# The second input projection of a two-layer encoder as one unrolled stream, with its normalisation read back and its head scales on ScalarE

## What is computed

```python
def odd_layer(x, g_pre, g_post, w_in, q_norm, k_norm, w_out):
    ...
    h = rms_norm(x, g_pre)
    proj = jnp.einsum('btd,de->bte', h, w_in)
    q, k, v, gate = jnp.split(proj, SPLIT_C, axis=-1)
    q = rms_norm(q.reshape(B, T, C_HEADS, C_HEAD_DIM), q_norm)
    k = rms_norm(k.reshape(B, T, C_KV_HEADS, C_HEAD_DIM), k_norm)
    v = v.reshape(B, T, C_KV_HEADS, C_HEAD_DIM)
    q = jnp.concatenate([rope(q[..., :half], rows), rope(q[..., half:], cols)], axis=-1)
    k = jnp.concatenate([rope(k[..., :half], rows), rope(k[..., half:], cols)], axis=-1)
    q = q.reshape(B, T, C_KV_HEADS, C_HEADS // C_KV_HEADS, C_HEAD_DIM)
    o = block_attention(q, k, v, C_HEAD_DIM ** -0.5).reshape(B, T, C_WIDTH)
    y = jnp.einsum('bte,ed->btd', o * jax.nn.silu(gate), w_out)
    return x + rms_norm(y, g_post)
```

## Time and profile before

| | us |
|---|---|
| median of 3 runs | 2465.69 (2465.58 to 2466.36) |
| the profiled execution | 2463.42 |
| its span in the trace | 2461.6 |
| PE busy in the span | 2148.5 (87%) |
| DVE, ACT, POOL busy | 1582.5, 991.0, 1124.1 |
| granted PE clock, mean | 0.928 |

### The profile page before, as it was taken

How to read it: one execution, slowest core, us unless ns; L and a number is a source line. 1 busy time by engine, 2 the same in 40 slices (tenths; PEclk the granted TensorE clock), 3 DMA queues, 4 the chain that set the end, 5 groups by cost and what they waited for, 6 DMA issues and landing times. The chain is left out here.

```text
span 2461.6 us, 25658 instructions
## 1 busy us (share of the span) xinstructions
PE 2148.5 (87%) x9420; PEld 1600.6 (65%) x9420; DVE 1582.5 (64%) x1980; ACT 991.0 (40%) x1259; POOL 1124.1 (46%) x580
## 2 busy tenths in 40 slices
PE   6999988959999999958952987998699999996895
PEld 4777867847777766636742765787466666663674
DVE  7264156756776666625658999995377777773565
ACT  5132133213555566533323232210066666664331
POOL 5333443423555565523126767543266666663300
PEclk9999999977999999978976998999799999998898
DMA  4133487246555554244332222221623232313434
GB/s 154 35 118 129 128 295 192 73 118 126 116 117 112 115 114 99 59 133 140 99 106 83 78 94 98 82 94 65 149 50 82 65 75 65 73 39 112 157 103 128
DMA packets 223272, 262.75 MB, mean 107 GB/s; under 512 B 137440, under 2 KB 147040, under 8 KB 223152
## 3 DMA queue, kind: packets, MB, share of 16 engines
q1 hardware_dynamic: 223152, 261.17, 38.2%
HBM read 162.62 MB, written 98.50 MB: 106 GB/s over the span
## 5 line engine op out<-in xcount | busy, mean ns | idle before, releaser
L1689 POOL TENSOR_TENSOR c_PL<-c_PF,c_PH 128x1024 fp32r<-128x1024 f32 x128 | 307.0, 2399 | 199.1 <-ACT c_PH L1553 142.2
L1689 POOL TENSOR_TENSOR ab_PL<-ab_PF,ab_PH 128x1024 fp32r<-128x1024 f32 (+3 forms) x128 | 269.1, 2102 | 237.1 <-ACT ab_PH L1553 178.8
L1550 ACT ACTIVATE ab_PF<-ab_SA 128x1024 f32<-128x1024 f32 (+3 forms) x160 | 143.6, 897 | 243.6 <-PE ab_SA L1409 143.1
L1550 ACT ACTIVATE c_PF<-c_SA 128x1024 f32<-128x1024 f32 x160 | 164.3, 1027 | 168.7 <-PE c_SA L1444 168.7
L1601 DVE TENSOR_REDUCE c_MH<-c_SM 128x1 f32<-128x512 f32 x256 | 172.9, 688 | 85.2 <-PE c_SM L1374 83.6
L847 PE MATMUL e_acc<-e_XH,e_wh 128*128 128x512 f32 x480 | 197.8, 412 | 25.6 <-DVE e_XL_r L1016 16.1
L340 PE MATMUL p_acc<-XH,p_wh 128*128 128x512 f32 x432 | 186.4, 431 | 26.3 <-POOL Y_r L174 26.3
L847 PE MATMUL e_acc<-e_XL_r,e_wh 128*128 128x512 f32 x480 | 193.5, 403 | 0.0
L847 PE MATMUL e_acc<-e_XH,e_wl 128*128 128x512 f32 x480 | 193.4, 403 | 0.0
L340 PE MATMUL p_acc<-Y_r,p_wh 128*128 128x512 f32 x432 | 172.2, 399 | 0.0
L340 PE MATMUL p_acc<-XH,p_wl 128*128 128x512 f32 x432 | 172.1, 398 | 0.0
(11 more groups left out here) (255 smaller groups left out, 5569.9 us busy)
## 6 DMA issues: line engine op xcount, KB each, us to landing
o_G<-silu_gate SPq DMA_DIRECT2D x48, 256.0 KB, 2.8
c_Q<-qC_hi SPq DMA_DIRECT2D x32, 384.0 KB, 5.4
e_raw<-in_w_tiles SPq DMA_DIRECT2D x20, 512.0 KB, 3.8
p_raw<-in_w_tiles SPq DMA_DIRECT2D x18, 512.0 KB, 3.6
o_WL<-in_w_out SPq DMA_DIRECT2D x16, 512.0 KB, 5.6
e_XL<-in_xT SPq DMA_DIRECT2D x12, 512.0 KB, 9.8
silu_gate<-e_ta SPq DMA_DIRECT2D x24, 256.0 KB, 2.0
ab_Q<-qA_hi SPq DMA_DIRECT2D x16, 384.0 KB, 5.6
```

Source lines behind the costliest of these rows:

```text
L1550: nc.scalar.activation(used(PF[p], h, s), used(SA, h, s), ACT.Exp).then_inc(e_done, 1)
L1689: nc.gpsimd.tensor_tensor(used(PL[p], h, s), used(PF[p], h, s), used(PH[p], h, s).bitcast(F32), ALU.subtract).then_inc(p_lo[0], 1)
```

## The change

`project` is gone and a new function `inner` takes its place. It is written like `entry`: plain Python lists of units, no hardware loops.

- `output_projection` 0 no longer works out the next layer's norm, and ends as `output_projection` 1 does. `inner` does not take `Y` from SBUF. It loads x from `x_mid`, splits the raw values and sums the squares as `entry` does; the norm enters when DVE moves a unit out of PSUM (L1131 of after).
- The first six units take the first two weight tiles with the three chunks as they arrive. The head sums of unit 0 come after unit 6. From there two are done after each odd unit and one after each even one, until they run one unit behind.
- The head scale is ACT's: Ln of the mean square (L1032), then Exp with factor -0.5 (L1035). There is no reciprocal on DVE for it.
- POOL multiplies a weight tile by the gain once, in place (L856); ACT rounds it (L1001), POOL subtracts (L864).
- The values are made in one pass over four weight pieces of 512, all 12 token tiles in six banks, and stand before the gates. Their token scales are 12 small matmuls into the bank of unit 28, copied out by DVE.
- A gate unit works as in `entry`.

```diff
@@ output_projection, the next layer's norm
-                    square_sum("y", p)
-                if t == 4 and x is not None:
-                    square_sum("n", x)
+                    square_sum(p)
...
-                if p is not None and t >= 2 and nxt:
...
-                    nc.scalar.activation((nsq if k else nsq_sum)[:], YF[:, k, cols(p)], ACT.Square
-                                         ).then_inc(n_sq, 1)
...
-                    nc.vector.reciprocal(rstd_next[:, cols(x)], rstd_next[:, cols(x)]).then_inc(next_ready, 1)
@@ inner, the units and their sums
+    U = [(tiles[t], t, c) for c in range(NC) for t in range(2)]
+    U += [(tiles[t], t, c) for t in range(2, 10) for c in range(NC)]
+    U += [(("value", i), V0 + 3, i) for i in range(TT // 2)]
+    U += [(gates[t], G0 + t, c) for t in range(KT) for c in range(NC)]
...
+    sums_after, done = [[] for n in range(N)], 0
+    for n in range(6, v0):
+        sums_after[n] = [m for m in range(done, done + 1 + n % 2) if m < n]
+        done += len(sums_after[n])
@@ inner, SyncE: loads, then stores, in this order
+            for n in range(N):
+                for w in begins[n]:
+                    if w + 2 < len(W):
+                        load(w + 2)
+                for m in sums_after[n]:
+                    store(m)
...
@@ inner, GpSimd
+            for n in range(N):
+                for w in splits[n]:
+                    scaled(w)
+                    low_weights(w)
+                if n == 5:
+                    rotate(0)
+                for m in sums_after[n]:
+                    rotate(m + 1)
...
@@ inner, TensorE
+            for n in range(N):
...
+                    wait_count(pe, acc_read, n - 5)
+                    products(n)
+                if n in (1, 3, 5):
+                    x_square_sum(n // 2)
+                for m in sums_after[n]:
+                    head_sums(m)
+                if n == v0 - 1:
+                    token_scales()
@@ inner, ScalarE
+            def square(n):
...
+                act.wait_ge(acc_read, n + 1)
+                wait_count(act, q_sum, i - 1)
+                nc.scalar.activation(tsq[i % 2][:], ta[i % 3][:], ACT.Square).then_inc(q_sq, 1)
+
+            def head_scale(n):
...
+                act.wait_ge(q_sum, i + 1)
+                wait_count(act, r_norm, i - 1)
+                nc.scalar.activation(tsd[i % 2][:], sums[i % 2], ACT.Ln, bias=epst[:], scale=1.0 / HD
+                                     ).then_inc(q_log, 1)
+                act.wait_ge(q_log, i + 1)
+                nc.scalar.activation(tsd[i % 2][:], tsd[i % 2][:], ACT.Exp, scale=-0.5).then_inc(q_rstd, 1)
...
+            for n in range(N):
+                for w in splits[n]:
+                    high_weights(w)
...
+                for m in sums_after[n]:
+                    square(m + 1)
+                    head_scale(m)
+                    high(m)
...
@@ inner, VectorE: evict(n) = scale from PSUM and swap; finish(n) = add, multiply, subtract
+                nc.vector.tensor_tensor(ta[s][:], bank(n), rstd[:, cols(c)], ALU.mult).then_inc(acc_read, 1)
...
+                nc.vector.tensor_tensor(ta[s][:], ta[s][:], tb[s][:], ALU.add).then_inc(r_sum, 1)
...
+                dve.wait_ge(q_rstd, i + 1)
+                nc.vector.tensor_tensor(ta[s][:], ta[s][:], tsd[i % 2][:], ALU.mult).then_inc(r_norm, 1)
...
+                dve.wait_ge(hi_done, i + 1)
+                nc.vector.tensor_tensor(sl[stage_of(n)][:].bitcast(F32R), ta[s][:], sh[stage_of(n)][:], ALU.subtract
+                                        ).then_inc(lo_done, 1)
...
+            for n in range(N):
+                if n == v0:
+                    finish(n - 1)
+                evict(n)
...
+                if n - 1 in qk and n != v0:
+                    finish(n - 1)
+                if n == 8:
+                    prepare(2)
```

More of the change, by code:

```diff
@@ L1692, in _, with output_projection @@
                     bias_low(h + 1)
-def output_projection(nc, ar, l, S, A, Y, rstd_next, gpost, ones, epst, xin, xout):
+def output_projection(nc, ar, l, S, A, Y, gpost, ones, epst, xin, xout):
     tag = f"o{l}"
-    nxt = rstd_next is not None
     row0 = 16 * l
@@ L1812, in _ @@
             load_w(1)
-            for period, t, g, a, p, x in stages():
+            for period, t, g, a, p in stages():
                 if g is not None:
@@ L1841, in _, with square_sum @@
                                         ).then_inc(w_lo, 1)
-            if nxt:
-                for c in range(NC):
-                    for k in range(1, KT):
-                        pool.wait_ge(n_sq, c * KT + k + 1)
-                        wait_count(pool, n_added, c * (KT - 1) + k - 1)
-                        nc.gpsimd.tensor_tensor(nsq_sum[:], nsq_sum[:], nsq[:], ALU.add).then_inc(n_added, 1)
         @block.tensor
         def _(pe):
-            def square_sum(kind, c):
-                i = sums_order.index((kind, c))
-                wait_count(pe, sd_ready, i)
-                pe.wait_ge(y_added if kind == "y" else n_added, (c + 1) * (KT - 1))
-                nc.tensor.matmul(sums[:], ones[:], (sq_sum if kind == "y" else nsq_sum)[:], start=True, stop=True
-                                 ).then_inc(sum_ready, 1)
+            def square_sum(c):
+                wait_count(pe, sd_ready, c)
+                pe.wait_ge(y_added, (c + 1) * (KT - 1))
+                nc.tensor.matmul(sums[:], ones[:], sq_sum[:], start=True, stop=True).then_inc(sum_ready, 1)
             pe.wait_ge(sel_set, 1)
             pe.wait_ge(rz_in, 32)
-            for period, t, g, a, p, x in stages():
+            for period, t, g, a, p in stages():
                 if g is not None:
@@ L1889, in high_weights, with deviation @@
                 nc.scalar.activation(WH[:, t, :], WF[:, t, :], ACT.Copy).then_inc(w_hi, 1)
-            def deviation(kind, c):
-                act.wait_ge(sum_ready, sums_order.index((kind, c)) + 1)
-                if kind == "y":
-                    wait_count(act, y_ready, c * KT)
-                out = rstd[:] if kind == "y" else rstd_next[:, cols(c)]
-                nc.scalar.activation(out, sums[:], ACT.Sqrt, bias=epst[:], scale=1.0 / D).then_inc(sd_ready, 1)
+            def deviation(c):
+                act.wait_ge(sum_ready, c + 1)
+                wait_count(act, y_ready, c * KT)
+                nc.scalar.activation(rstd[:], sums[:], ACT.Sqrt, bias=epst[:], scale=1.0 / D).then_inc(sd_ready, 1)
             act.wait_ge(z_rcp, 1)
@@ L1929, in _ @@
                 if t == 0 and p is not None:
-                    deviation("y", p)
-                if t == 4 and x is not None:
-                    deviation("n", x)
+                    deviation(p)
         @block.vector
@@ L2030, in build_trunk @@
         with ar.scope() as s1:
-            output_projection(nc, ar, 1, S, A, s1.both("Y1", [P, KT, T]), None, gpost[1], ones, epst, S["X1"], A["yT"])
+            output_projection(nc, ar, 1, S, A, s1.both("Y1", [P, KT, T]), gpost[1], ones, epst, S["X1"], A["yT"])
 def set_up(nc, ar, ones, epst, gpre, gpost, A):
```

786 lines of the change are left out of this document (372 added, 414 removed).

## The result

The changed kernel takes 2468.9 us (median of 18 runs, 2464.7 to 2474.7), the kernel before in the same comparison 2463.7 (18 runs, 2458.9 to 2470.1). The ratio is 1.0020, with a 95% interval from 1.0012 to 1.0029, so 3.0 to 7.1 us slower. The forecast was 6.0 us slower; the medians differ by 5.1. The profiled execution has a span of 2465.0, against 2461.6.

A forecast was written before the change was run, and what follows sets the result against it. DVE was read as bounding the old qk units, a closed ACT-DVE ring the new. 1366 + 212 + 39 + 133.5 + 12.1 put attention "c" at 1762.6, 6.0 later than 1756.55; with the median 2465.7 this gave 2471.7 us, range 2462 to 2481.

The forecast's parts named there:

- The end of the output projection: Block 0 ends as block 1 does; new block's first load at 1287 instead of 1306.36, a gain of 19.
- The first units: Start of new block, modelled on entry: unit 6 ends at 1359, second round begins at about 1366.
- The ring: Qk units: closed chain over ACT and DVE, square to next square, with two table loads; 7.4 us a plain ring.
- term for weight work: Qk rings with weight tiles: POOL and DVE meet, 1.4 us for each of 7 tiles, 9.8 in all.
- the two tables: Two table products standing once in the qk ring, at unit 8; 2.5 us.
- first meeting: Rings with a weight tile: DVE's multiply waits for POOL's weight scaling and loses about 0.95 us.
- Values, gates, end: After the qk rounds: values 39 us, 24 gate units 133.5, last matmul to attention "c" 12.1.
- (B): Rival: POOL and DVE don't meet on the ring, bare hand-overs, gates at 5.46; 9.4 us earlier, 2456.3; chance 0.22.
- second meeting: Rings with weight work: POOL's weight subtraction pushes the next rotation to 5.1 into the ring, another 0.45 us.
- (C): Rival: a table switch costs another 1.28 us waiting for an empty pipeline; 69 us more, 2541; chance 0.04.
- (D): Rival: PE, at 1.2 GHz after idling in weight rings, becomes the bound; 24 us more, 2496; chance 0.13.
- (E): Rival: table loads hidden or not executed, PE bounds at 6.35 a unit; 2420 to 2431 us; chance 0.03.

The follow-up runs named there:

- aligned: Changed kernel with its three small tiles (token scales, 0/1 matrix, head gains) allocated last; ratio 0.9999 against the kernel before.
- fourloads: Changed kernel with a one-column Exp and Ln added between Ln and Exp, making four table loads a unit; 2554.2 us, ratio 1.0368 against the kernel before.
- noload: Changed kernel with the head scale's Ln made an Exp, so no table loads between square and Exp; ratio 0.9855 against the kernel before.
- reorder: Changed kernel with ACT's rounding and DVE's subtraction of a unit moved one stage later; 2435.2 us, ratio 0.9883 against the kernel before.
- dvescale: Changed kernel with the root on ACT and the reciprocal back on DVE between add and multiply; ratio 1.0075 against the kernel before.
- rsqrt: reorder with small tiles last, in entry too, and Abs_reciprocal_sqrt on ACT replacing Ln and Exp; 2414.7 us, ratio 0.9800 against the kernel before.

## Why the prediction came out right, point by point

**The end of the output projection.** Forecast 1287, measured 1287.32. Reading it from block 1, which ends in the form that block 0 was to take, was sound. That it came out to 0.3 is luck of the execution: in the nine other kernels that share everything ahead of this point, the load starts between 1281.5 and 1290.9.

**The first units.** The second round began at 1364.29 (forecast 1366). Most of the difference is ahead of the first head sum, which started at 1357.71; unit 6 was forecast to end at 1359.

**The ring.** The mechanism was right, and experiments bear it out from three sides: without loads, with twice the loads, and with the two steps at its end moved away. The plain ring was 0.13 too short in the forecast (hand-overs), 3.5 over 27 rounds. The term for weight work was twice too large: 12.3 were set for seven tiles and the two tables, and measured were 209.3 - 27 x 7.53 = 6.0. The step that failed there is the second half of it, "POOL's weight subtraction then pushes the next rotation to 5.1, another 0.45", and "about 0.95" for the first meeting. The pushed rotation ran only 0.18 into the multiply and cost it 0.05 to 0.09, and the first meeting cost 0.69. Besides, six tiles lay in the rounds, not seven, and the round with the two table products was 1.3 longer than plain, not 2.5. The two errors partly cancel, and they are as large as the effect: with a plain ring of 7.4, as forecast, attention "c" would have begun at 1759.6 - 3.5 = 1756.1, where it began before. So the chain and its size were understood, but that the sign came out right is in part luck. In all attention "c" came 3.0 earlier than forecast: 1.7 at the start of the rounds, 2.7 in them, 0.5 at the values, less 1.7 at the gates and 0.2 at the end.

**Values, gates, end.** Values 38.5 for 39. Gates were mis-sized by 1.7: between 5.46 and 5.62 the forecast took the middle, but the new code shares the layout of `entry`, and went at its 5.62 (by `aligned` it is the tiles' places that make the difference). End 12.3 for 12.1.

**The rivals.** (B), no meeting of POOL and DVE, was half true: the second meeting cost next to nothing. The time lies between its price and the forecast. (C), a dearer switch, is refuted by `fourloads`. (D), PE at 1.2 GHz as the bound: PE did fall to it after long idle times, as in the earlier trace rows, and idled 42 us at head sums, but no move of DVE waited for it in the rounds. A head sum of the changed kernel in the first rounds, timeline of PE:

```profile
1388.40 2.08 PE L927 MATMUL n_ssb<-n_tsq,n_headsel 128*128 128x512 f32 x2 [7.02 <-ACT n_tsq L1025]
```

(E), loads off the ring, is refuted by `noload`, though its time was the right one for a kernel without loads: 2420 to 2431 forecast, 2426.1 measured.

**Where the gain went.** One comparison in the prediction is misread: "before, 27 units took 212.2". The stretch from 1353.10 to 1565.30 holds 672 matmuls of products, so 28 units, and the head sums of all 30. It begins with the head sum of unit 0, while the rounds of the new block are counted from the square of unit 2. The forecast doesn't rest on it, but "starts later than the old one (round 1 at 1366, not 1353)" does. Like is compared with like at DVE's multiply, for the first and the 29th unit, before and after:

```profile
1360.84 0.69 DVE L488 TENSOR_TENSOR p_ta<-p_ta,p_tsd 128x512 f32<-128x512 f32 x1
...
1574.27 2.27 DVE L488 TENSOR_TENSOR p_ta<-p_ta,p_tsd 128x512 f32<-128x512 f32 x1
```

```profile
1361.50 0.69 DVE L1145 TENSOR_TENSOR n_ta<-n_ta,n_tsd 128x512 f32<-128x512 f32 x1 [6.01 <-ACT n_tsd L1035]
...
1578.31 0.69 DVE L1145 TENSOR_TENSOR n_ta<-n_ta,n_tsd 128x512 f32<-128x512 f32 x1 [3.37 <-ACT n_tsd L1035]
```

The block starts 19.0 earlier, but the first multiply comes 0.7 later. So the 19 us won ahead of the block are gone before the rounds begin: x is loaded, split and squared here, and seven units are made before the first head sum (1357.71), where the old kernel had made two (1353.12). How much each of the two costs is not shown. The pace is then 7.74 a unit where it was 7.62, and the 29th multiply comes 4.0 later. Some 14 won at the values pay for gates that are 4.2 longer, a tail that is 4.9 longer and about 4 of overlap between the last qk units and what follows them, with 1 us left over. That makes the 3.1 by which attention "c" begins later.

The change frees DVE of 3.35 a unit, and the half-empty DVE row shows that it did. The pace gains nothing from it: before, DVE served three units in turn and was full; now ACT and DVE wait for each other, with one unit at a time at its end. `reorder` shows that this order is the limit. `dvescale` parts the change in two: the new stream with the reciprocal on DVE is 0.75% slower than the kernel before, and the head scale on ACT brings that to 0.20%. The head scale on ACT in the old order of three units in turn was not tried.

## What to carry to other kernels

When work is moved from a full engine to one with room, write down the chain of one item with every step that stands ahead of the next item's first step in some queue, and compare its length with the old bound. If the moved work only changes places within that chain (3.35 of reciprocal for 3.29 of loads and Exp), its plain length stays, and here only the rings in which DVE was held up gained. Moving the last steps of an item behind the first of the next took 1.5 off a plain ring here and was worth 1.4%. An operation that is slowed by a neighbour costs only what isn't covered: the same add of 1.8 was free beside table loads and cost over 1 us ahead of a reciprocal.

## What the runs showed of the hardware that was not expected

- The place of tiles in SBUF changes the step of 128x512 matmuls: 234, 232 and 227 ns (5.622, 5.575 and 5.440 for 24) at the same granted clock of 1.00. Small tiles allocated in the middle shift all behind them. Putting them last was worth 0.2% in one block and 0.6% in two.
- Four table loads a unit, two of them behind an operation of one column, took 1.28 each, with 0.02 ahead and behind (`fourloads`). No wait for an empty pipeline shows.
- POOL's products are held up by DVE as well as the other way round: the sine product took 1.26 in the changed kernel and 1.74 behind an add in `rsqrt`.
- PE's lead matters: in `noload`, with PE on unit 7 when DVE moves unit 2, 27 rounds ran at 6.13 a round although the moves are 6.48 apart where they wait for PE.
